# Moving the slots of the split weights to eight different remainders modulo 256 bytes in a two-block float32 model on one core

## What is computed

```python
def first_block(x, ...):            # two times
    h = rms_norm(x, g_pre)
    parts = split_cols(h @ w_in)    # 1024 x 2816, then three kinds of attention
    mixed = concatenate([o_a, o_b, o_c]) * silu(z)
    x = x + rms_norm(mixed @ w_out, g_post)

def second_block(x, ...):           # two times
    x = layer_norm(ALPHA * x + 0.5 * swiglu(x, gate1, up1, down1))   # hidden width 2816
    h = x @ w_in_2                  # 1024 x 2560, then pooling and a gated recurrence
    x = layer_norm(ALPHA * x + mix @ w_out_2)
    x = layer_norm(ALPHA * x + 0.5 * swiglu(x, gate2, up2, down2))
```

## Time and profile before

| what | value |
|---|---|
| runs shown, device time | 2533.08 and 2537.02 us, median 2535.05 us |
| the profiled execution, from its first to its last instruction | 2537.3 us |
| TensorE, matmuls (PE) | 2443.8 us busy, 96% of the span, 13142 instructions |
| TensorE, weight loads (PEld) | 1961.0 us, 77% |
| VectorE (DVE) | 1294.5 us, 51% |
| ScalarE (ACT), GpSimd (POOL) | 659.9 us and 650.7 us, 26% each |
| mean granted TensorE clock | 0.983 of full speed |

### The profile page before, as it was taken

One profiled execution on the slowest core, in us unless ns is written; L12 is line 12 of the kernel. 1 busy time (PEld: TensorE's weight loads), 2 busy tenths in 40 slices (PEclk: granted clock), 3 DMA queues, 4 the chain that ended last, 5 costly groups with the idle time before them and its releaser, 6 DMA issues. The chain is left out here.

```text
span 2537.3 us, 34388 instructions
## 1 busy us (share of the span) xinstructions
PE 2443.8 (96%) x13142; PEld 1961.0 (77%) x13142; DVE 1294.5 (51%) x1918; ACT 659.9 (26%) x1331; POOL 650.7 (26%) x510
## 2 busy tenths in 40 slices
PE   8999999997999999998999999999999998999997
PEld 6776677665888887886888887888887886888885
DVE  5557475566433345877433335333345877433344
ACT  3036331461211102533311102211102543211101
POOL 2016410282333212003333212333212003333211
PEclk9999999998999999999999999999999999999998
DMA  6220232102232321312232331332322312233322
GB/s 252 67 96 18 67 123 67 34 10 74 91 97 93 113 94 66 107 47 76 90 98 93 115 102 61 100 97 93 116 91 67 100 44 83 84 98 99 118 92 78
DMA packets 58088, 222.69 MB, mean 88 GB/s; under 512 B 6340, under 2 KB 8532, under 8 KB 57724
## 3 DMA queue, kind: packets, MB, share of 16 engines
q1 hardware_dynamic: 53712, 206.87, 24.9%
q10 hardware_dynamic: 4268, 14.33, 1.5%
HBM read 219.05 MB, written 5.80 MB: 89 GB/s over the span
## 5 line engine op out<-in xcount | busy, mean ns | idle before, releaser
L180 DVE CAST two_hi<-two_raw 128x1024 fp32r<-128x1024 f32 (+1 forms) x292 | 219.2, 751 | 895.1 <-PE bank L249 887.7
L242 PE MATMUL bank<-xh,two_hi 128*128 128x512 f32 x1728 | 429.6, 391 | 0.2 <-ACT sg L1591 0.2
L249 PE MATMUL bank<-xl,two_hi 128*128 128x512 f32 x1728 | 428.3, 390 | 0.0
L245 PE MATMUL bank<-xh,two_lo 128*128 128x512 f32 x1728 | 426.8, 389 | 0.0
L182 DVE TENSOR_TENSOR two_lo<-two_raw,two_hi 128x1024 fp32r<-128x1024 f32 (+1 forms) x292 | 405.4, 1388 | 10.0
L249 PEld LDWEIGHTS bank<-xl,two_hi 128*128 128x128 f32 x1728 | 324.8, 188 | 67.4
L245 PEld LDWEIGHTS bank<-xh,two_lo 128*128 128x128 f32 x1728 | 324.4, 188 | 67.5
L242 PEld LDWEIGHTS bank<-xh,two_hi 128*128 128x128 f32 x1728 | 323.0, 188 | 68.4 <-issue 1.3
L1611 POOL TENSOR_TENSOR hm<-sg,hm 128x512 f32<-128x512 f32 x88 | 193.6, 2200 | 558.6 <-ACT hm L1594 558.6
L242 PE MATMUL bank<-hh,two_hi 128*128 128x512 f32 x704 | 171.8, 392 | 0.0
L249 PE MATMUL bank<-hl,two_hi 128*128 128x512 f32 x704 | 171.4, 390 | 0.0
(11 more groups left out here) (276 smaller groups left out, 2958.7 us busy)
## 6 DMA issues: line engine op xcount, KB each, us to landing
two_raw<-in_up SPq DMA_DIRECT2D x180, 512.0 KB, 3.7
two_raw<-in_down SPq DMA_DIRECT2D x64, 704.0 KB, 4.1
one_raw<-in_w_in SPq DMA_DIRECT2D x44, 512.0 KB, 3.7
two_raw<-in_w_in SPq DMA_DIRECT2D x40, 512.0 KB, 3.6
one_raw<-in_w_out SPq DMA_DIRECT2D x16, 512.0 KB, 3.7
two_raw<-in_w_out SPq DMA_DIRECT2D x16, 512.0 KB, 3.7
w<-in_w ACTq DMA_DIRECT2D x2, 2048.0 KB, 18.3
x<-in_x SPq DMA_DIRECT2D x4, 512.0 KB, 7.2
```

Of the source, the lines that this page charges most:

```text
L180: v.tensor_copy(st.hi[:, h, 0:w], st.raw[:, r, 0:w]).then_inc(st.hi_made, 1)
L242: pe.matmul(out[:], st.hi[:, slot, k * P:(k + 1) * P], xh[:, h * kp + k, :], start=h == 0 and k == 0, stop=False)
L245: pe.matmul(out[:], st.lo[:, slot, k * P:(k + 1) * P], xh[:, h * kp + k, :], start=False, stop=False)
L249: mm = pe.matmul(out[:], st.hi[:, slot, k * P:(k + 1) * P], xl[:, h * kp + k, :], start=False, stop=h == pieces - 1 and k == kp - 1)
```

## The change

Each slot of `hi` and of `lo` is 16 floats (64 bytes) longer than the weights in it, and unused tiles stand before, between and after the two rings. The instructions take `0:width` of a slot, so they move as many bytes as before. The rest of the program is as before; everything that is allocated behind the rings lies 512 bytes higher, and the tile `held` is 512 bytes longer to keep the place of the second block's tiles.

```diff
@@ -86,6 +86,7 @@
 LINE = 64
+SLOT_REST = 16
@@ -123,10 +124,16 @@
-    def allocate_parts(self, ctx, tag=""):
-
-        self.hi = ctx.enter_context(self.nc.sbuf_tensor(f"{self.tag}{tag}_hi", [P, HL_RING, self.width], F32R))
-        self.lo = ctx.enter_context(self.nc.sbuf_tensor(f"{self.tag}{tag}_lo", [P, HL_RING, self.width], F32R))
+    def allocate_parts(self, ctx, before, between, after):
+
+        def skip(name, n):
+            if n:
+                ctx.enter_context(self.nc.sbuf_tensor(f"{self.tag}_{name}", [P, n], F32))
+        skip("parts_before", before)
+        self.hi = ctx.enter_context(self.nc.sbuf_tensor(f"{self.tag}_hi", [P, HL_RING, self.width + SLOT_REST], F32R))
+        skip("parts_between", between)
+        self.lo = ctx.enter_context(self.nc.sbuf_tensor(f"{self.tag}_lo", [P, HL_RING, self.width + SLOT_REST], F32R))
+        skip("parts_after", after)
@@ -411,9 +418,10 @@
-    v.tensor_copy(st.hi[:, h, :], st.raw[:, r, :]).then_inc(st.hi_made, 1)
+    w = st.width
+    v.tensor_copy(st.hi[:, h, 0:w], st.raw[:, r, :]).then_inc(st.hi_made, 1)
     v.wait_ge(st.hi_made, n + 1)
-    v.tensor_tensor(st.lo[:, h, :], st.raw[:, r, :], st.hi[:, h, :].bitcast(F32), ALU.subtract).then_inc(st.w_split, 1)
+    v.tensor_tensor(st.lo[:, h, 0:w], st.raw[:, r, :], st.hi[:, h, 0:w].bitcast(F32), ALU.subtract).then_inc(st.w_split, 1)
@@ -492,7 +500,7 @@
-        kit.stream.allocate_parts(ctx)
+        kit.stream.allocate_parts(ctx, 32, 8, 24)
@@ -2439,7 +2447,7 @@
-            kit.two.allocate_parts(later)
+            kit.two.allocate_parts(later, 0, 8, 56)
@@ -2456,7 +2464,7 @@
-            c1.enter_context(nc.sbuf_tensor("held", [P, (135552 - 66432) // 4], F32))
+            c1.enter_context(nc.sbuf_tensor("held", [P, (136064 - 66432) // 4], F32))
```

## The result

| what | before | after |
|---|---|---|
| device time, median | 2535.05 us | 2577.93 us (2576.71 and 2579.14) |
| ratio, 95% interval | | 1.0177 [1.0161, 1.0193] |
| profiled execution | 2537.3 us | 2574.9 us |

The changed kernel is slower by 1.8% (the two medians alone stand 42.9 us or 1.7% apart). That is under the 2% that I took as the line between a change and none, but far beyond the interval, and outside the range of the prediction, which ended at 2550 us.

A forecast was written before the change was run, and what follows sets the result against it. TensorE's pitch of 226.7 ns over 9120 matmuls was taken as the bound; TensorE, VectorE, GpSimd and moved tiles each added 0 to 2537.3 us, 2535 us as a median, range 2520 to 2550, chance 0.85 of within 2%.

The forecast's parts named there:

- What bounds the kernel, and that only the pitch could matter: Whole kernel: 9120 matmuls at 0.2267 us make 2067 us, 81% of the span; only moving that pitch matters over 2%.
- I take 0, because of two rows: TensorE's split-weight matmuls: VectorE's traffic leaves the pitch unchanged and out-of-step operands cost nothing in the trace, so 0 us.
- A memory in which equal remainders collide should show at least one of these.: TensorE: colliding remainders should show as a pitch disturbed by VectorE's traffic or a price for out-of-step operands; supported 0.
- rival A: TensorE: equal remainders cost the 11.7 ns, so 6560 matmuls drop to 215 ns, 77 us less, 2458 us; chance 0.08.
- The matmuls that change: TensorE: 5120 matmuls in `two`, where hi slot 0 stays at remainder 0, and 1440 in `one`; together 6560.
- the slowest piece without a stall: Mixers, line 242: eight matmuls take 2.09 us in place of 1.98, 15.7 ns each; times 6560, a loss of 103 us.
- rival B: TensorE: equal remainders keep the pitch down; offset starts lose 77 us (2612 us), by the bound 103 us (2638 us); chance 0.07.
- the 7.7 ns: TensorE: 51 us / 6560 matmuls, the loss for each from which a slowdown decides; anything below was counted to the forecast.
- rival C: VectorE's casts or subtractions take 10% more or less; mixers pass on up to 8 us, 2527 to 2543; within forecast's 0.85.
- GpSimd: Six subtractions after LayerNorms end 1.8 us before TensorE resumes; one 75% longer would still be hidden, so 0 us.
- What would show it wrong: Dense products: the forecast is wrong if any steady piece differs from 1.98 us by over 0.05 us.
- The alternation of tiles: Second block: tiles alternate between two lengths, pieces of 1.90 us if offsets gain or about 2.06 if they lose, except hi 0.

## Why the prediction was wrong

- *What bounds the kernel, and that only the pitch could matter.* Right. The whole change is in the pitch of 9120 matmuls, and instructions, loads, casts and subtractions kept their number and length.
- *TensorE.* This is the step that failed: "I take 0, because of two rows". The matmuls out of step that show no price are plain float32 products, which take 430 ns for 512 columns where ours take 226.7. No run moves their operands against each other. The plain float32 matmuls that a run does move so are the transposes of line 1010 (1018 after the edit), whose `lg_ring` operand stands 64 bytes higher in the run with the moving operands alone: their starts are 109 ns apart (the median) either way. And in the stretches at half the clock, matmuls of split weights start 427 ns apart (the median) in the kernel before, with the weights at 64 and with them at 224 and 96 alike. The cost was seen only with `fp32r` operands at the full clock, and of that the trace of before had not one matmul out of step. Rows of another kind of product were no bound for this one. In place of 0 the runs showed 5.2 ns for each of the 9120 matmuls, 47.4 us in the traces and 42.9 us in the medians.
- *"A memory in which equal remainders collide should show at least one of these."* The argument excluded only the sign of rival A. Equal remainders are the fast case, and that VectorE doesn't disturb TensorE says nothing on TensorE's own two operands.
- *The matmuls that change.* I counted 6560, since slot hi 0 of the second block keeps its remainder. In fact it is slowed as well, by the state that the pieces before it leave for several matmuls: its `xl` pieces take 2.00 us. The high product with `xh` in that slot has medians of 236, 224, 231, 236, 228, 232 and 231 ns.
- *The slow piece of the earlier trace rows.* I called the eight matmuls of 2.09 us "the slowest piece without a stall" and spread their 0.11 us over seven distances, 15.7 ns each. In the trace these distances are 314, 229, 233, 236, 224, 231 and 236 ns. The first holds 87 of the 116 ns and the other six average 231.5 ns, 4.8 above the pitch. So the slow state stood in the trace of the kernel before. Priced by those six, B would have cost 4.8 x 6560 = 31 us, or 4.8 x 9120 = 44 us for all split products. That the latter lies so near to the 43 us measured is partly luck, since the six belong to a stream that settles and not to an offset. It also contradicts what I held for rival A, that the gap is the same at every one of the matmuls.
- *The price of rival B.* What the runs show is B: equal remainders keep the pitch down. That it is the meeting of two reads is not shown. I priced it at 11.7 ns for each (77 us), up to 15.7 (103 us). An offset of 64 costs 233.3 - 226.7 = 6.6 ns, the change's mixture 47.4 us / 9120 = 5.2 ns on average, and 42.9 us in the medians. That is below the 7.7 ns that I had named as the point from which B decides, so a B at its true size would have stood at 2578 us, inside "within 2%" and outside my range. Taking only 0 and 77 us as outcomes, and a range that reached 15 us up, was the second fault: the bounds of the unknown cost stood 77 us below and 103 us above, and no row spoke for a bound against a value halfway to it.
- *Rival A* is wrong: no distance brought the mean pitch below 226.7 ns.
- *VectorE (rival C) and GpSimd.* Right: VectorE's cast and subtraction keep their medians of 694 and 1226 ns, and GpSimd's subtraction takes 2354 ns in place of 2356.
- *What would show it wrong.* A steady piece was to differ by over 0.05 us. Those shown of the changed kernel take 2.00 to 2.03 in place of 1.98 us, so this sign all but fails to see the 43 us: 0.05 us is 7 ns for each matmul, more than the 5.2 that the change costs. The alternation of tiles was foreseen and came, weaker.

The Trainium skill (TensorE: Matmul & The Clock Gate, step 1 of "Step-by-step: what each phase is for") says that loading the next weights takes no read bandwidth from the running matmul. I drew from it that no placement can change the pitch, and the runs disagree with that for these operands at the full rate: the same loads and matmuls cost 6.6 ns more for each matmul when only their distance changes. The Trainium skill's formula for the gap (the same page, "Back-to-back issue gap"), 215.8 ns for 512 columns, was reached by `fp32r` matmuls at none of the distances; the best is 226.7. The section gives that formula for the isolated gap, and for a stream of loads and matmuls of 512 columns about 131 ns, which no such matmul here comes near. The prediction took the first for a matmul of this stream.

## What to carry to other kernels

Where TensorE streams `fp32r` operands of 512 columns back to back with a load before each, let stationary and moving operands begin at the same remainder modulo 256 bytes, in every tile and every ring slot: 2533 to 2537 us here (medians and single times) against 2542 to 2589 for the eleven other layouts. Before pricing an alignment from rows, ask whether those rows are the same kind of product at the same rate, and take a slow piece apart, distance by distance, before calling it an average. And when one unknown term is multiplied by 9120, let the range hold the values between its bounds, not only zero.

## What the runs showed of the hardware that I had not expected

- The mean pitch of `fp32r` matmuls of 128 x 512 at the full clock depends on the distance between stationary and moving operand, modulo 256 bytes: 226.7 ns at 0 bytes, 230.7 at 8, 231.1 at 16, 233.3 at 32 and 64, 234.2 at 96, 232.6 at 128, 229.0 at 192, 233.3 at 224, 228.0 at 240, 233.3 at 248. Moving both alike changes nothing (ratio 1.0002 [0.9992, 1.0012]).
- There is a memory: after a product at distance 64 a product in step takes three to six matmuls to return to 227 ns. After a break by other matmuls, with all operands in step, the kernel before takes eight of them (the piece at 893.74 us).
- At half the clock the distance costs nothing (427 ns at 0, 64, 96 and 224). For plain float32 the traces have one case, transposes that keep their 109 ns with one operand moved by 64 bytes.
- Halving the load's columns doesn't lower the pitch, and in the first block, in step, it raises it from about 227 to 230 ns.
